# Memory tokens laid out transposed, multiplied before they are normalised, with x turned in between

## The reference, cut to what matters

```python
def rms_norm(x, g):
    y = x * lax.rsqrt(jnp.mean(x * x, axis=-1, keepdims=True) + EPS)
    return y * g
h = rms_norm(x, norm_mix_pre)            # x (512, 1024)
z = h @ w_in                             # q, k, v, qx, pin and gates are cut from z
mkv = rms_norm(mem, norm_mem) @ w_mem_kv # mem (256, 1024), w_mem_kv (1024, 1024)
mk, mv = jnp.split(mkv, 2, axis=-1)      # keys and values of 4 heads of 128
s = einsum('bshd,bmhd->bhsm', qx, mk) * 128 ** -0.5; p = softmax(s)
ox = einsum('bhsm,bmhd->bshd', p, mv)
```

## Time and profile before

| | us |
|---|---|
| three runs | 815.83, 816.45, 812.82 (median 815.83) |
| the profiled execution | 812.71 |
| its span, first to last instruction | 810.9 |
| TensorE busy in it | 799.6 |
| VectorE, ScalarE, GpSimd busy | 465.4, 356.4, 47.7 |

### The profile page before, as it was taken

One profiled execution on the slowest core, in us unless ns is written; L12 is line 12 of the kernel. 1 busy time (PEld: TensorE's weight loads), 2 busy tenths in 40 slices (PEclk: granted clock), 3 DMA queues, 4 the chain that ended last, 5 costly groups with the idle time before them and its releaser, 6 DMA issues.

```text
span 810.9 us, 11900 instructions
## 1 busy us (share of the span) xinstructions
PE 799.6 (99%) x4672; PEld 693.5 (86%) x4672; DVE 465.4 (57%) x624; ACT 356.4 (44%) x632; POOL 47.7 (6%) x100
## 2 busy tenths in 40 slices
PE   7999999999999999999999999999999999999997
PEld 6988777777788888888888899999999999888885
DVE  4742565566443432623755598888888887833222
ACT  6632545546444423234433464444444445622111
POOL 1100000144000000000001220000000000000000
PEclk9999999999999999999999999999999999999999
DMA  9543221311221332234462013333333344641011
GB/s 320 168 143 111 69 87 53 96 62 53 68 89 53 105 98 71 92 104 156 155 219 74 20 53 105 104 103 103 103 103 103 103 129 146 217 154 54 1 52 53
DMA packets 67786, 84.21 MB, mean 104 GB/s; under 512 B 3217, under 2 KB 61089, under 8 KB 67746
## 3 DMA queue, kind: packets, MB, share of 16 engines
q1 hardware_dynamic: 67712, 83.65, 31.5%
q10 hardware_dynamic: 34, 0.01, 0.0%
HBM read 81.54 MB, written 2.11 MB: 103 GB/s over the span
## 4 chain that ended last, share of the span: by engine, by line
PE 96%; DVE 2%; DMA 1%; ACT 1%; issue 0%; POOL 0%; SPq 0%; DVEq 0%; POOLq 0%; ACTq 0%
PE pair L1206 89%; PE pair L1298 1%; PE pair L1281 1%; PE pair L1308 1%; PE pair L1288 1%; PE pair L1213 1%; PE pair L1312 1%; DMA g_mem_b<-in_norm_mem 1%; PE pair L1234 0%; DVE mem_in L872 0%; ACT square L608 0%; DVE y L872 0%; DVE w_lo L368 0%; PE pair L1329 0%; DVE x L1041 0%
## 5 line engine op out<-in xcount | busy, mean ns | idle before, releaser
L368 DVE TENSOR_TENSOR w_lo<-raw,w_hi 128x1024 fp32r<-128x1024 f32 x69 | 85.3, 1237 | 96.7 <-ACT w_hi L363 96.5
L1206 PE MATMUL pair<-hT_hi,w_hi 128*128 128x512 f32 x336 | 136.5, 406 | 0.0
L1206 PE MATMUL pair<-hT_lo,w_hi 128*128 128x512 f32 x336 | 131.3, 391 | 0.0
L1206 PE MATMUL pair<-hT_hi,w_lo 128*128 128x512 f32 x336 | 131.3, 391 | 0.0
L363 ACT ACTIVATE w_hi<-raw 128x1024 fp32r<-128x1024 f32 x70 | 73.9, 1056 | 90.8 <-PE pair L1206 82.9
L1206 PE MATMUL pair<-T_hi,op_hi 128*128 128x256 f32 x320 | 90.6, 283 | 0.0
L1206 PE MATMUL pair<-T_lo,op_hi 128*128 128x256 f32 x320 | 90.6, 283 | 0.0
L1206 PE MATMUL pair<-T_hi,op_lo 128*128 128x256 f32 x320 | 90.6, 283 | 0.0
L1206 PEld LDWEIGHTS pair<-hT_hi,w_hi 128*128 128x128 f32 x336 | 63.1, 188 | 14.0
L1206 PEld LDWEIGHTS pair<-hT_hi,w_lo 128*128 128x128 f32 x336 | 63.1, 188 | 13.9
L1206 PEld LDWEIGHTS pair<-hT_lo,w_hi 128*128 128x128 f32 x336 | 63.2, 188 | 12.0
(11 more groups left out here) (185 smaller groups left out, 1582.0 us busy)
## 6 DMA issues: line engine op xcount, KB each, us to landing
raw<-in_w_in SPq DMA_DIRECT2D x42, 512.0 KB, 4.8
raw<-in_w_ffn_up SPq DMA_DIRECT2D x22, 512.0 KB, 4.8
raw<-in_w_ffn_gate SPq DMA_DIRECT2D x22, 512.0 KB, 4.3
raw<-in_w_ffn_down SPq DMA_DIRECT2D x22, 512.0 KB, 4.1
raw<-in_w_mem_kv SPq DMA_DIRECT2D x8, 512.0 KB, 7.2
raw<-in_w_branch_a SPq DMA_DIRECT2D x8, 512.0 KB, 4.1
raw<-in_w_out SPq DMA_DIRECT2D x8, 512.0 KB, 4.1
x_in<-in_x SPq DMA_DIRECT2D x4, 512.0 KB, 9.7
```

The costliest lines, as they stand in the source:

```text
L368: eng.tensor_tensor(lo, raw_view(s), hi.bitcast(F32), ALU.subtract).then_inc(weights_split, 1)
L1206: ins = pe.matmul(dst, a, b, start=first and n == 0, stop=last and n == 2, skip_group_check=onto)
```

## The change

The host now hands `mem` over transposed (1024 on the partitions, in 8 blocks of 128, by 256 tokens), and both norm weights as 128x8 columns.

- Memory: ACT and DVE split `memT_in` straight from SBUF, block by block, with the norm weight as a column scale (8 pieces of 128x256 each). It is multiplied unnormalised; 1/rms of a token comes in later. Squares are taken by ACT in turns 6 and 7 (two of 128x1024), DVE adds the eight blocks (128x1024, 128x512, 128x256) in turn 8, TensorE sums over partitions (`mem_sum`, two matmuls of one column, behind the tile of step 8), DVE moves that to `meansq`, POOL makes 1/rms, DVE writes two diagonal matrices in turn 10, TensorE spreads them by a product with ones (`mem_scale`, two matmuls of 128 columns, behind the tile of step 10), DVE scales `mk` in turn 11. The values are scaled by 1/rms as they leave PSUM.
- Removed: the 512 KB load of `g_mem_b`, the row norm of mem, its 16 transposes and 4+4 evictions, the spread of the other norm weight and its copy. `WARM_UP` is 40.
- Steps: memory 4, 5, 6, 7, 0, 1, then k, v, then memory 2, 3, then q. k is step 6 instead of 8.
- x: squares of blocks 0 and 1 in ACT's turn 2, of 2 and 3 in turn 3; DVE normalises (scale 1/rms alone, the weight later) blocks 0, 1 in turn 3 and 2, 3 in turn 4. TensorE transposes by column blocks, 0 to 3 behind step 4 and 4 to 7 behind step 5, each piece over all four row blocks, so the first waits until all four are normalised.
- Queue of SP: the small weight column, half of memT, half of chunk 0, the other halves, chunk 1, x 0 and 1, chunk 2, x 2 and 3, chunk 3.
- `rel_row` moves from DVE's turn 7 to turn 8, behind the sum of squares.

```diff
-WARM_UP = (30, 0, 3)
-X_AFTER = (2, 3, 5, 6)
+WARM_UP = 40
+X_SQUARES = {2: (0, 1), 3: (2, 3)}
+X_NORMS = {3: (0, 1), 4: (2, 3)}
+X_TURNS = (4, 5)
+MEM_SUM = 8
...
-    steps = [[("mem", h)] for h in range(2 * X_HEADS)]
+    steps = [[("mem", h)] for h in (4, 5, 6, 7, 0, 1)]
     steps += [[("k", 0)], [("v", 0)]]
+    steps += [[("mem", 2)], [("mem", 3)]]
     steps += [[("q", j)] for j in range(8)]
...
+    steps[MEM_SUM].append(("mem_sum", 0))
+    steps[MEM_SUM + 2].append(("mem_scale", 0))
...
-            for m in range(MT):
-                sp.dma_start(mem_in[:, m, :], mem[P * m:P * m + P, :]).then_inc(mem_loaded[m], 16)
-            sp.dma_start(g_mem_b[:, :], row_bcast(g_mem)).then_inc(gain_loaded["mem"], 16)
-            load_chunk(0)
+            sp.dma_start(g_mem_c[:, :], g_mem).then_inc(gain_loaded["mem"], 16)
+            for h, signal in enumerate((half_in, raw_in[0])):
+                sp.dma_start(memT_in[:, 4 * h:4 * h + 4, :], mem_t[:, 4 * h:4 * h + 4, :]).then_inc(mem_loaded[h], 16)
+                load_half(0, h, signal)
             load_chunk(1)
-            for t in range(TT):
-                sp.dma_start(x_in[:, t, :], x[P * t:P * t + P, :]).then_inc(x_loaded[t], 16)
+            load_x(0)
+            load_x(1)
+            load_chunk(2)
+            load_x(2)
+            load_x(3)
...
+            for h, (loaded, n, done_hi) in enumerate(((half_in, 16, half_hi), (raw_in[0], 16, weights_hi))):
+                act.wait_ge(mem_loaded[h], 16)
+                for k in range(4 * h, 4 * h + 4):
+                    act.activation(memT_hi[:, k, :], memT_in[:, k, :], ACT.Copy, scale=g_mem_c[:, k:k + 1])\
+                       .then_inc(mem_hi_done, 1)
+                act.wait_ge(loaded, n)
+                ks = slice(4 * h, 4 * h + 4)
+                act.activation(split_at(0)[0][:, ks, :], raw_view(0)[:, ks, :], ACT.Copy).then_inc(done_hi, 1)
+            split_hi(act, 1)
...
-                if s < TT:
-                    act.wait_ge(x_loaded[s], 16)
-                    mean_square(x_in[:, s, :], NORM_X + s, square0[:, :])
+                for t in X_SQUARES.get(s, ()):
+                    act.wait_ge(x_loaded[t], 16)
+                    mean_square(x_in[:, t, :], NORM_X + t, square0[:, :])
+                if s in (MEM_SUM - 2, MEM_SUM - 1):
+                    h = s - MEM_SUM + 2
+                    act.activation(mem_sq[:, 4 * h:4 * h + 4, :], memT_in[:, 4 * h:4 * h + 4, :], ACT.Square)\
+                       .then_inc(mem_squared, 1)
...
                 while done < stream_upto(s):
                     split_lo(dve, done)
                     done += 1
-                if s < TT:
-                    norm_rows(x_in[:, s, :], x_in[:, s, :], NORM_X + s, g_mix_pre_b[:, :])
+                for t in X_NORMS.get(s, ()):
+                    dve.wait_ge(rstd_ready, NORM_X + t + 1)
+                    dve.tensor_scalar(x_in[:, t, :], x_in[:, t, :], rstd[:, NORM_X + t:NORM_X + t + 1], None, ALU.mult)\
+                       .then_inc(rows_normed, 1)
...
+                        elif t in merged_no:
+                            mem_evicted(t)
+                if s == MEM_SUM:
+                    mem_sum_of_squares()
+                if s == MEM_SUM + 2:
+                    mem_diagonal()
+                if s - 1 == X_TURNS[0]:
+                    turned_x(0)
+                if s == 8:
...
+            def mem_sum_of_squares():
+                for h in range(2):
+                    dve.wait_ge(mem_squared, h + 1)
+                for n in (4, 2, 1):
+                    ins = dve.tensor_tensor(mem_sq[:, 0:n, :], mem_sq[:, 0:n, :], mem_sq[:, n:2 * n, :], ALU.add)
...
-            def turn_rows(src, e):
-                pe.wait_ge(rows_normed, e // 2 + 1)
-                if E_MEM <= e:
+            def turn_x(e):
+                pe.wait_ge(rows_normed, TT)
+                if e >= 4:
                     pe.wait_ge(turned_split, e - 3)
-                turn_to(bk(4 + e % 4), src)
+                for t in range(TT):
+                    ins = pe.transpose(bk(4 + e % 4)[:, P * t:P * t + P], x_in[:, t, P * e:P * e + P], ident[:, :])
+                ins.then_inc(rows_turned, 1)
...
+                if kind == "mem_sum":
+                    pe.wait_ge(mem_summed, 1)
+                    for m in range(MT):
+                        ins = pe.matmul(dst[:, m:m + 1], mem_sq[:, 0, P * m:P * m + P], inv_d[:, :], start=True, stop=True)
...
+                if kind == "mem_scale":
+                    pe.wait_ge(diag_ready, MT)
+                    for m in range(MT):
+                        ins = pe.matmul(dst[:, P * m:P * m + P], ones[:, :], diag[:, m, :], start=True, stop=True)
...
-                if s in X_AFTER:
-                    t = X_AFTER.index(s)
-                    for h in range(2):
-                        turn_rows(x_in[:, t, 512 * h:512 * h + 512], E_MEM + 2 * t + h)
+                if s in X_TURNS:
+                    b = X_TURNS.index(s)
+                    for e in range(4 * b, 4 * b + 4):
+                        turn_x(e)
```

More of the change, by code:

```diff
@@ L213, in encoder_block @@
     ident = sb("ident", 206, [P, P])
[L214 removed]
+    ones = sb("ones", 196, [P, P])
     small_at = [206.5]
@@ L261, in encoder_block @@
         raw_in = [sem(f"raw_in{i}") for i in range(2)]
-        mem_loaded = [sem(f"mem_loaded{i}") for i in range(MT)]
+        mem_loaded = [sem(f"mem_loaded{i}") for i in range(2)]
         x_loaded = [sem(f"x_loaded{i}") for i in range(TT)]
@@ L460, in _ @@
             sp.dma_start(scale_p[:, :], pool_scale).then_inc(smalls_loaded, 16)
-            for c in range(2, 6):
+            for c in range(3, 6):
                 load_chunk(c)
@@ L555, in inverse_rms @@
                     .then_inc(rstd_ready, 1)
-            for n in range(MT + TT):
+            for n in range(TT):
                 inverse_rms(n)
+            pool.wait_ge(tile_merged, merged_no[("mem_sum", 0)])
+            for m in range(MT):
+                c = NORM_MEM + m
+                pool.tensor_tensor(rstd[:, c:c + 1], meansq[:, c:c + 1], minus_half[:, :], ALU.pow).then_inc(mem_rstd_ready, 1)
             pool.wait_ge(rows_turned, E_V)
@@ L876, in turn_lo, with turned_x @@
                 dve.wait_ge(turned_hi, e + 1)
[L877 to L882, removed]
+                dve.scalar_tensor_tensor(out=turned_at(e, False), in0=bk(4 + e % 4), scalar=g_pre_c[:, e:e + 1],
+                                         in1=turned_at(e, True).bitcast(F32), op0=ALU.mult, op1=ALU.subtract)\
+                   .then_inc(turned_split, 1)
+            def turned_x(b):
+                dve.wait_ge(gain_loaded["pre"], 16)
+                for e in range(4 * b, 4 * b + 4):
+                    turn_lo(e)
             def maxima(u):
@@ L964, in merged_lo, with mem_evicted @@
                 dve.wait_ge(mrg_split, j + 1)
-            dve.wait_ge(gain_loaded["mem"], 16)
[L967 to L972, removed]
-            hi, lo = split_at(0)
-            for h, signal in enumerate((half_split, weights_split)):
-                if h == 1:
-                    turn_lo(2)
+            def mem_evicted(t):
+                kind, i = t
+                n = tile_no[t]
+                src = bk(n % 4)
+                dve.wait_ge(tile_full, n + 1)
+                if kind == "mem_sum":
+                    c = NORM_MEM
+                    dve.tensor_scalar(meansq[:, c:c + MT], src[:, 0:MT], 1.0, EPS, ALU.mult, ALU.add).then_inc(tile_merged, 1)
+                else:
+                    dve.wait_ge(tile_copied, copied_no[("mem", X_HEADS - 1)])
+                    scale = ap(src, 0, [list(src.ap[0]), [0, X_HEADS], [1, N_MEM]])
+                    dve.tensor_tensor(mk[:, :, :], mk[:, :, :], scale, ALU.mult).then_inc(tile_merged, 1)
@@ new lines, in mem_sum_of_squares, with mem_diagonal @@
+            def mem_sum_of_squares():
+                for h in range(2):
+                    dve.wait_ge(mem_squared, h + 1)
+                for n in (4, 2, 1):
+                    ins = dve.tensor_tensor(mem_sq[:, 0:n, :], mem_sq[:, 0:n, :], mem_sq[:, n:2 * n, :], ALU.add)
+                    if n > 1:
+                        link(ins)
+                    else:
+                        ins.then_inc(mem_summed, 1)
+            def mem_diagonal():
+                for m in range(MT):
+                    dve.wait_ge(mem_rstd_ready, m + 1)
+                    dve.tensor_scalar(diag[:, m, :], ident[:, :], rstd[:, NORM_MEM + m:NORM_MEM + m + 1], None, ALU.mult)\
+                       .then_inc(diag_ready, 1)
@@ new lines, in _ @@
+            dve.wait_ge(gain_loaded["mem"], 16)
+            hi, lo = split_at(0)
+            for h, (hi_done, signal) in enumerate(((half_hi, half_split), (weights_hi, weights_split))):
+                for k in range(4 * h, 4 * h + 4):
+                    dve.wait_ge(mem_hi_done, k + 1)
+                    dve.scalar_tensor_tensor(out=memT_lo[:, k, :], in0=memT_in[:, k, :], scalar=g_mem_c[:, k:k + 1],
```

(7 more changed lines are left out.)

125 lines of the change are left out of this document (60 added, 65 removed).

## The result

| | before | changed |
|---|---|---|
| median of the runs (us) | 815.11 | 822.82 |
| lowest and highest | 812.82, 816.45 | 821.06, 823.26 |
| profiled execution, its span | 812.71, 810.9 | 823.13, 820.5 |
| TensorE busy, its share of the chain | 799.6, 96% | 801.9, 93% |

The changed kernel is slower: ratio 1.0096, 95% interval 1.0077 to 1.0116, or 7.7 us by the medians. The forecast was 822.0.

The account below looks back on a forecast made before the run. TensorE bounds the kernel (busy 799.6 of 810.9 us, 96% of the chain). Start -4.5, waits +5.7, +1.95 and +2.2, new work +0.65, rest rounding: +6.2 on the median 815.83 gives 822.0, range 816.5 to 826.5.

Parts of the forecast that it names:

- The start: First memory work: without the removed load and row norms, step 1 starts at 13.2 instead of 17.7, 4.5 us gained.
- Step 4: Memory step behind chunk 2, forecast to land at 19.6: TensorE runs it from 21.95 to 24.8.
- x: Behind step 4: transposes wait until all four x blocks are normalised at 30.5, a TensorE stall of 5.7 us.
- The clock: Rival at the x wait: TensorE's clock falls in the stall, 1.6 us more, 823.6 in all; chance 0.25.
- (a): The rival of the falling clock: +7.8, 823.6, chance 0.25; its sign is transposes of x at 421 ns.
- mem_sum: Behind step 8: TensorE waits 1.95 us for DVE's sum of squares, queued behind step 10's split; one-column matmuls 0.2.
- mem_scale: Behind step 10: TensorE waits 2.2 us for diagonals held by rel_row, SP's queue and the split of a late chunk.
- The sum: Start of step 11, the second q tile: 65.6 instead of 59.38, 6.2 us later, giving 822.0.
- Only the x wait real: Rival (b): the mem_sum and mem_scale waits, 4.1 us, fall away; +2.1, 817.9; chance 0.10.
- The x wait covered: Rival (c), behind step 4: no x stall, the start's 4.5 stands against 0.65 of work; -3.9, 811.9; chance 0.09.
- No earlier start: Rival (d), at the start: chunk 0 lands at 11.9 as before, all moves by 1.5; +7.7, 823.5; chance 0.11.

Follow-up runs that it names:

- the repeated run: The changed kernel measured once more with nothing altered, beside the others on one chip: median 823.14 us, ratio 1.0099 to the kernel before.

## Why the prediction was right, point by point

- **The start.** Forecast: step 1 at 13.2, a gain of 4.5. In the trace of after its first matmul is near 13.0, a gain of 4.7. ACT took the second half of chunk 0 at 10.1 (forecast 10.4), but what it had waited for was another transfer: the second half of `memT_in` landed at 8.46, and its four splits, which the forecast had put into the waits at no cost, kept ACT until about 10.1, while the half of chunk 0 landed at about 9.95 (issued 2.66, 7.3 to landing). The two ended within 0.2 us of each other, so the number holds. The run with the load put back moved both transfers and shows only that transfers set the start.
- **Step 4.** I had its split ready as step 3 ends. Chunk 2 landed at 20.3 instead of 19.6, and TensorE stood 0.9 (22.79 for its first matmul). Off the path: x was later still.
- **x.** Forecast: rows normalised at 30.5, a wait of 5.7. Measured: 31.18 and 5.3. The order of the chain (chunk 2, split, squares, split, squares, split, norms) is as worked out, to 0.7 us, all of it chunk 2's. The one-tensor product took 0.70 (two in 1.41), as the copy's row had it. The Trainium skill, "VectorE: DVE Perf Modes", section "Mode 2×_2P", has a float32 operation with one tensor from SBUF run at twice the rate of one with two, and this trace agrees: with two tensors the same size took 1.22.
- **The clock.** I gave it 0.25 as a rival and 1.6 us. It fell, in the profiled execution twice, and the first fall cost 2.7. This is the term that was mis-sized: v ended at 51.15 instead of 47.8, 0.7 by chunk 2 and 2.7 by the clock. I priced only 3.2 us at half rate; the rate was half from 29.6 to 36.4, and from 31.2 on there was work. The transposes of x took 421 ns each, the sign given for (a). The 272 ns in rows 9 are of transposes begun ahead of the idle 2.30; those behind it have 272 in the trace too. And the 421 ns at the old kernel's start stand beside a granted clock of 1.00, so there the low level is read from the durations alone; the 421 ns of x stand beside 0.50.
- **mem_sum.** Wait 1.95 forecast, 2.0 measured; its two narrow products 0.2 forecast, 0.58 measured.
- **mem_scale.** Wait 2.2 forecast; 1.8 in the repeated run, and in the first trace covered by the low clock. The chain over `rel_row`, SP, chunk 6 and the split of step 12 is as worked out: sum done 4.7 after v's end (4.85), chunk 6 there at 12.5 after it (12.9), diagonals at 15.2 (15.6). From v's end to step 11: 17.8 forecast, 17.8 measured; that they are equal is partly luck, as 1.6 of low clock lay where the wait would have been.
- **The sum.** In the profiled executions the shift is 9.6, not 6.2; the missing 3.4 are the clock's 2.7 and chunk 2's 0.7. That the forecast still came out 0.8 from the measured median is partly luck. The shift was worked out against the old kernel's profiled execution and then added to its median, which is 3.1 higher; the changed kernel's profiled execution (823.13) lies at its own median (822.82) and has no such 3.1. So 3.4 too little in the shift and 3.1 too much in the base nearly cancel. The old kernel's executions had spans of 810.6 to 817.3, with lower clocks for the longer, so its profiled one (810.9) was among its quickest. The ends of the range, 816.5 and 826.5, don't follow from its terms one by one.
- **Time outside the span.** The forecast has no term for it. An execution of the old kernel takes 1.7 to 1.9 us more than its span in every run whose span is on record; the changed kernel's four behind the forecast took 2.5 to 3.5 more. So about 1 us of the 7.7 lies outside the span, ahead of the first instruction or behind the last. It is there in most executions of the variants too, but not in those of the two kernels with filled waits (1.8 in all 14). Its cause stays open.
- **The rivals.** Only the x wait real: no, each of the other two is worth about 2 us. The x wait covered: no. No earlier start: no.

## What to carry to other kernels

An earlier start was worth nothing here until the operands of the later steps kept up with it. So walk each engine's program in its order from the new start, and look above all at what stands ahead of the needed instruction on its engine. Small work (a sum of squares, a table of biases) put ahead of or behind a split can hold a whole transfer queue and, through it, the matrix engine. When TensorE has to stand, fill the wait, and judge a change by pairs of runs with the clock held, because a wait and a low clock can hide one another.

## What the runs showed of the hardware

- The granted clock fell to half in all four traces with the wait of 5.3 unfilled, but not at the same point of it: at 28.2, 29.6 and 30.0 while TensorE stood, and in the repeated run only at 31.1, as it began to work again. The transposes and step 5 lost 1.9 to 2.9 us by it. The Trainium skill, "TensorE: Matmul & The Clock Gate", Part 1, has an idle array return to 1.2 GHz; the three falls during the 5.3 agree.
- It also fell behind much shorter waits, when TensorE was at work again: behind the 2.0 ahead of mem_sum in three of four traces (the first, `rel_row` in turn 7, x earlier), and behind the 2.9 with the load put back. It held behind a 2.0 in the repeated run and behind the 2.2 ahead of the transposes. What decides between them the runs don't show.
- What held it was work nobody reads: 65 transposes, of 0.11 each, gave back about 2 us at step 11.
- Two float32 products of a single column took 0.34 to 0.61 between other work, and 0.87 where the clock fell meanwhile; they aren't free.
